# The mask of a block-causal attention moved from VectorE into the score matmuls, with a shifted schedule, in a float32 encoder block

## The reference

```
h = rms_norm(x); proj = h @ w_in
# A: 16 heads of 64, 2 kv heads, a window of two 64-token chunks, a sink per head, rotary
out_a = swa_sink_attention(rope(a_q), rope(a_k), a_v, sinks) * silu(a_g)
# B: 8 heads; q and kv from normed latents of 512 and 256; rotary part of 64 shared
s = (q_nope . k_nope + q_rope . k_rope) * scale
s = where(key_chunk <= query_chunk, s, -1e30)       # chunks of 64
out_b = softmax(s) @ v * silu(b_g)
y = rms_norm(x + concat(out_a, out_b) @ w_out) * final_norm_w
```

## Time and profile before

| | us |
|---|---|
| median of three runs | 681.09 (681.01 to 681.31) |
| the profiled execution | 681.09 |
| its span, first to last instruction | 679.3 |
| TensorE busy | 668.8 |
| VectorE, ScalarE, GpSimd busy | 336.6, 305.5, 307.2 |
| TensorE's granted clock, mean | 0.998 |

### The profile page before, as it was taken

One profiled execution on the slowest core, in us unless ns is written; L12 is line 12 of the kernel. 1 busy time (PEld: TensorE's weight loads), 2 busy tenths in 40 slices (PEclk: granted clock), 3 DMA queues, 4 the chain that ended last, 5 costly groups with the idle time before them and its releaser, 6 DMA issues.

```text
span 679.3 us, 8915 instructions
## 1 busy us (share of the span) xinstructions
PE 668.8 (98%) x3196; PEld 559.2 (82%) x3196; DVE 336.6 (50%) x596; ACT 305.5 (45%) x574; POOL 307.2 (45%) x149
## 2 busy tenths in 40 slices
PE   8999999999999999999999999999999999999995
PEld 7888888888888888888888888888888888888884
DVE  6857132988784635645554577778651100101013
ACT  7723231311343664565465466676753321313233
POOL 0044443354253532542443645556966584464720
PEclk9999999999999999999999999999999999999999
DMA  8632322223232212222321412102025732233225
GB/s 332 234 108 95 109 93 94 94 95 108 76 94 94 93 63 94 93 77 80 113 78 62 151 64 94 63 31 95 32 94 179 285 124 93 93 99 107 73 77 203
DMA packets 21878, 73.54 MB, mean 108 GB/s; under 512 B 2385, under 2 KB 2641, under 8 KB 21713
## 3 DMA queue, kind: packets, MB, share of 16 engines
q1 hardware_dynamic: 18144, 65.61, 28.4%
q10 hardware_dynamic: 3696, 7.43, 3.0%
HBM read 68.83 MB, written 4.19 MB: 108 GB/s over the span
## 4 chain that ended last, share of the span: by engine, by line
PE 91%; DVE 4%; ACT 2%; issue 1%; DMA 1%; SPq 0%; ACTq 0%; DVEq 0%
PE bank L1084 28%; PE bank L1080 28%; PE bank L1083 28%; PE bank L1212 1%; PE bank L1222 1%; PE bank L1331 1%; DVE bank L944 1%; DVE pb L953 1%; DVE t L909 1%; DMA xs<-x_t 1%; DVE ptb_lo L958 1%; PE bank L1234 1%; PE bank L1235 1%; PE bank L1100 1%; PE bank L1103 1%
## 5 line engine op out<-in xcount | busy, mean ns | idle before, releaser
L283 POOL TENSOR_TENSOR w_lo<-w_raw,w_hi 128x1024 fp32r<-128x1024 f32 x100 | 242.3, 2428 | 312.9 <-ACT w_hi L369 312.9
L369 ACT ACTIVATE w_hi<-w_raw 128x1024 fp32r<-128x1024 f32 x110 | 116.2, 1056 | 208.3 <-PE bank L1080 173.4
L1080 PE MATMUL bank<-x_hi,w_hi 128*128 128x512 f32 x504 | 196.9, 391 | 0.0
L1084 PE MATMUL bank<-x_lo,w_hi 128*128 128x512 f32 x504 | 196.7, 390 | 0.0
L1083 PE MATMUL bank<-x_hi,w_lo 128*128 128x512 f32 x504 | 196.2, 389 | 0.0
L1084 PEld LDWEIGHTS bank<-x_lo,w_hi 128*128 128x128 f32 x504 | 94.6, 188 | 20.2
L1080 PEld LDWEIGHTS bank<-x_hi,w_hi 128*128 128x128 f32 x504 | 94.7, 188 | 18.9 <-DVE mixed L894 0.5
L1083 PEld LDWEIGHTS bank<-x_hi,w_lo 128*128 128x128 f32 x504 | 94.7, 188 | 18.5
L1080 PE MATMUL bank<-w_hi,mx_hi 128*128 128x512 f32 x256 | 100.5, 393 | 0.0
L1083 PE MATMUL bank<-w_hi,mx_lo 128*128 128x512 f32 x256 | 100.0, 391 | 0.0
L1084 PE MATMUL bank<-w_lo,mx_hi 128*128 128x512 f32 x256 | 99.8, 390 | 0.0
(11 more groups left out here) (209 smaller groups left out, 923.3 us busy)
## 6 DMA issues: line engine op xcount, KB each, us to landing
w_raw<-w_stream SPq DMA_DIRECT2D x110, 512.0 KB, 3.3
y<-x_nat ACTq DMA_DIRECT2D x4, 1024.0 KB, 9.8
out<-y SPq DMA_DIRECT2D x6, 512.0 KB, 3.1
xs<-x_t SPq DMA_DIRECT2D x4, 512.0 KB, 5.3
mixed<-x_t SPq DMA_DIRECT2D x4, 512.0 KB, 5.1
fw<-final_w ACTq DMA_DIRECT2D x1, 1024.0 KB, 18.0
cos_b<-tables ACTq DMA_DIRECT2D x2, 256.0 KB, 2.9
sin_b<-tables ACTq DMA_DIRECT2D x2, 256.0 KB, 3.2
```

Source lines behind the costliest of these rows:

```text
L283: pool.tensor_tensor(w_lo[:, s % HL, :], w_raw[:, s % RAW, :], w_hi[:, s % HL, :].bitcast(F32), ALU.subtract)\
L369: act.activation(w_hi[:, s % HL, :], w_raw[:, s % RAW, :], ACT.Copy).then_inc(w_hi_ready, 1)
L1080: ins = pe.matmul(dst, ah, bh, start=start, stop=False)
L1084: return pe.matmul(dst, ah, bl, start=False, stop=stop)
```

## The change

The mask moves to TensorE: a sixth matmul adds to the last 64 columns of a score the product of a bf16 identity and a bf16 tile of 128x64 that holds -1e30 in its first 64 rows. VectorE then only reduces to the negated maximum. The two constants are made in the start stage, and the older mask tile with its two memsets ahead of B's first rotation is gone. Beside that the tables shift: A's group 0 has its scores at half steps 4, 7, 9, 12; B's chunks, rotations and mixed halves move by a fill or two; the rotary table load moves from fill 2 to fill 1; and the low halves of the query latent go from GpSimd to VectorE.

```diff
-AT_SCORES = [{2: 0, 5: 1, 8: 2, 11: 3}] * 4
-AT_TRANSPOSE = [{5: 0, 8: 1, 11: 2, 14: 3}] * 4
-AT_PV = [{7: 0, 10: 1, 13: 2, 16: 3}] * 4
+AT_SCORES = [{4: 0, 7: 1, 9: 2, 12: 3}] + [{2: 0, 5: 1, 8: 2, 11: 3}] * 3
+AT_TRANSPOSE = [{7: 0, 9: 1, 12: 2, 14: 3}] + [{5: 0, 8: 1, 11: 2, 14: 3}] * 3
+AT_PV = [{9: 0, 11: 1, 14: 2, 16: 3}] + [{7: 0, 10: 1, 13: 2, 16: 3}] * 3
-LATENT_AT = {9: 0, 10: 1, 12: 2, 13: 3}
+LATENT_AT, LATENT_LOW_AT = {9: 0, 10: 1, 12: 2, 13: 3}, {9: (0,), 10: (1,), 13: (2, 3)}
-B_CHUNKS = [{2: (5,), 4: (6,), 10: (7,)}, {1: (8,), 3: (9,), 10: (10,)}, {1: (11,), 3: (12,), 10: (13,)},
-            {1: (14,), 4: (15,), 6: (16,), 8: (17,), 10: (18,)}]
+B_CHUNKS = [{1: (5,), 3: (6,), 10: (7,)}, {1: (8,), 3: (9,), 10: (10,)}, {1: (11,), 3: (12,), 10: (13,)},
+            {1: (14,), 2: (15,), 4: (16,), 7: (17,), 9: (18,)}]
-B_ROTARY = [{3: (0,), 4: (1, 2), 5: (3,), 6: (4,), 7: (5,)}] + [{2: (0,), 3: (1,), 4: (2, 3), 5: (4,), 6: (5,)}] * 3
+B_ROTARY = [{3: (0, 1), 4: (2,), 5: (3,), 6: (4,), 7: (5,)}] + [{2: (0, 1), 3: (2,), 4: (3,), 5: (4,), 6: (5,)}] * 3
-M_AT = {3: 2, 5: 3, 7: 4, 9: 5, 10: 6}
+M_AT = {2: 2, 4: 3, 5: 4, 7: 5, 9: 6}
@@ gpsimd: the low halves of the latent leave its loop of chunks
-                for k in {PB0 + AHEAD - 4: (0,), PB0 + AHEAD - 3: (1,), PB0 + AHEAD - 2: (2, 3)}.get(c, ()):
-                    pool.wait_ge(cqs_split, k + 1)
-                    pool.wait_ge(lat_lo, 2 + k)
-                    pool.tensor_tensor(cqs_lo[:, k, :], cq[:, k, :], cqs_hi[:, k, :].bitcast(F32), ALU.subtract).then_inc(lat_lo, 1)
@@ scalar
-                act.activation(B[4 + u % 2][:, 0:n], B[4 + u % 2][:, 0:n], ACT.Exp, bias=st_b[:, u % 4, 0:1], scale=-1.0,
+                act.activation(B[4 + u % 2][:, 0:n], B[4 + u % 2][:, 0:n], ACT.Exp, bias=st_b[:, u % 4, 0:1],
-                        if p == 0 and f == 2:
+                        if p == 0 and f == 1:
                             act.wait_ge(gated, 8)
@@ vector
+            dve.memset(mask_bf[:, :], 0.0).then_inc(consts_set, 1)
+            dve.wait_ge(consts_set, 3)
             dve.memset(v_t[:, 0:CHUNK], 0.0)
+            dve.memset(mask_bf[0:64, :], MASK_VALUE).then_inc(consts_set, 1)
             dve.wait_ge(tables_landed, 48)
+            dve.tensor_copy(ident_bf[:, :], ident[:, :]).then_inc(consts_set, 1)
+                    for k in LATENT_LOW_AT.get(hf, ()) if t == 3 else ():
+                        dve.wait_ge(cqs_split, k + 1)
+                        dve.tensor_tensor(cqs_lo[:, k, :], cq[:, k, :], cqs_hi[:, k, :].bitcast(F32), ALU.subtract).then_inc(lat_lo, 1)
-                sc = B[4 + u % 2][:, 0:n]
-                dve.tensor_tensor_reduce(sc, sc, mask_b[:, SEQ - n:], -1.0, 3e38, ALU.add, ALU.min, st_b[:, u % 4, 0:1]).then_inc(b_max, 1)
+                dve.reduce_max(st_b[:, u % 4, 0:1], B[4 + u % 2][:, 0:n], AX.X, negate=True).then_inc(b_max, 1)
-            dve.memset(mask_b[:, :], 0.0).then_inc(b_mask, 1)
-            dve.wait_ge(b_mask, 1)
-            dve.memset(mask_b[0:CHUNK, SEQ - CHUNK:], MASK_VALUE).then_inc(b_mask, 1)
@@ tensor
+            pe.wait_ge(consts_set, 6)
-                three(dst, qn_hi[par][:, h, q], qn_lo[par][:, h, q], kn_hi[par][:, h, 0:n], kn_lo[par][:, h, 0:n], False, True).then_inc(b_scores, 1)
+                three(dst, qn_hi[par][:, h, q], qn_lo[par][:, h, q], kn_hi[par][:, h, 0:n], kn_lo[par][:, h, 0:n], False, False)
+                pe.matmul(B[4 + w % 2][:, n - CHUNK:n], ident_bf[:, :], mask_bf[:, :], start=False, stop=True).then_inc(b_scores, 1)
```

More of the change, by code:

```diff
@@ L143, in build @@
         ident = at("ident", [P, P], F32, region(512))
[L144 to L147, removed]
+        ones = at("ones", [P, P], F32, region(512))
+        fold = at("fold", [P, P], F32, region(512))
         r_sums = region(512)
@@ L150, in build @@
         fold_r = at("fold_r", [P, P], F32R, r_sums)
+        ident_bf = at("ident_bf", [P, P], BF16, region(256))
+        mask_bf = at("mask_bf", [P, CHUNK], BF16, region(128))
         st_a = at("st_a", [P, 2, 6, 4], F32, region(192))
@@ L242, in build @@
         b_rot_evac, b_rot, b_rot_hi, b_rot_lo = sem("b_rot_evac"), sem("b_rot"), sem("b_rot_hi"), sem("b_rot_lo")
-        b_mask, b_scores, b_max, b_exp, b_recip, b_probs = sem("b_mask"), sem("b_scores"), sem("b_max"), sem("b_exp"), sem("b_recip"), sem("b_probs")
+        b_scores, b_max, b_exp, b_recip, b_probs = sem("b_scores"), sem("b_max"), sem("b_exp"), sem("b_recip"), sem("b_probs")
         b_turned, b_pt_hi, b_pt_lo, b_pv, b_out = sem("b_turned"), sem("b_pt_hi"), sem("b_pt_lo"), sem("b_pv"), sem("b_out")
@@ L319, in _ @@
             assert (KR0 + 2) % HL == 0
-            with pool.Fori((KR0 + 2) // HL, b_head // HL - 1) as i:
+            with pool.Fori((KR0 + 2) // HL, b_head // HL) as i:
                 for s in range(HL):
                     low_part(HL * i + s, s)
-            for c in range(b_head // HL * HL - HL, b_head):
+            for c in range(b_head // HL * HL, b_head):
                 low_part(c, c)
-                for k in {PB0 + AHEAD - 4: (0,), PB0 + AHEAD - 3: (1,), PB0 + AHEAD - 2: (2, 3)}.get(c, ()):
-                    pool.wait_ge(cqs_split, k + 1)
-                    pool.wait_ge(lat_lo, 2 + k)
-                    pool.tensor_tensor(cqs_lo[:, k, :], cq[:, k, :], cqs_hi[:, k, :].bitcast(F32), ALU.subtract).then_inc(lat_lo, 1)
             for ct in range(2):
@@ L706, in _ @@
             dve.tensor_tensor(sin_r[:, :], sin_r[:, :], rstd[:, :], ALU.mult).then_inc(consts_set, 1)
-            dve.wait_ge(consts_set, 4)
+            dve.wait_ge(consts_set, 7)
             def rotate_terms(src, cos, sin, count, evac=proj_evac):
@@ L964, in b_take @@
                 dve.tensor_tensor(m, B[7][:, :], m, ALU.mult).then_inc(b_out, 1)
-            dve.memset(mask_b[:, :], 0.0).then_inc(b_mask, 1)
-            dve.wait_ge(b_mask, 1)
-            dve.memset(mask_b[0:CHUNK, SEQ - CHUNK:], MASK_VALUE).then_inc(b_mask, 1)
             for part in range(6):
                 b_rotary(0, part)
-            dve.wait_ge(b_mask, 2)
             b_tile_low(5)
```

## The result

The changed kernel takes 688.62 us (median of four runs, 687.51 to 689.06) against 681.09 (681.01 to 681.31): ratio 1.0107, 95% interval 1.0090 to 1.0126. Slower was right, the size was not: +3.0 us forecast, +7.5 measured, outside the range of 682.0 to 685.8.

The account below looks back on a forecast made before the run. TensorE's queue was taken as the bound. Masks 3.3, less 1.7 of old waits, plus 0.6 (A group 0), 0.5 (fill 1) and 0.3 (last pair) made +3.0: 684.1 us, range 682.0 to 685.8.

Parts of the forecast that it names:

- Latent low halves: Four subtractions moved to VectorE in A, at most 0.69 us each: done 0.3 before TensorE asks, so no cost.
- Masks, 3.3: 32 extra mask matmuls on TensorE in B's scores, about 0.11 us each on the longer ones: 3.1 to 3.5 in all.
- rival 2: Next weight load does not wait for the mask, which steps only 0.037 us: +0.9, 682.0 us; chance 0.13.
- the prediction's own sign of being wrong: A step of 0.04 us behind the masks in TensorE's queue, or waits of B as large as before.
- Old waits, 1.7 back: Seven TensorE waits in B, 1.78 us in all: shorter VectorE chains, moved rotation parts and later TensorE recover 1.7.
- My 0.7 against 0.50: Score 6 of pair 2: chain gains 0.3 from the moved rotation part, four masks give 0.4, against a 0.50 wait.
- A group 0, 0.6: First A group's new schedule: two new TensorE waits of 0.3 us at transpositions 1 and 3; bounds 0 and 1.4.
- Fill 1 of pair 0, 0.5, and the last pair, 0.3: Work moved on ScalarE in B makes TensorE wait at transposition 1 of pair 0 and transposition 3 of the last pair.
- Output stage unchanged: After B, the output stage was expected to stay the same whether the forecast was right or wrong.
- Constants, nothing: Memsets and one 128x128 VectorE copy in the start stage: no cost; bounds 0 and 0.7.
- Rival 1: B is held by the VectorE and ScalarE chain, masks fall into its waits: -1.2, 679.9 us; chance 0.07.
- Rival 3: Work moved on ScalarE costs more than the moved rotation gives, waits at upper bounds: +4.7, 685.8 us; chance 0.17.

Follow-up runs that it names:

- e1: Changed kernel with the four latent low halves back on GpSimd: 683.50 us, against 681.36 for the kernel before beside it.
- e2: Changed kernel with the latent low halves still on VectorE but at later half steps (11 and 14): 683.60 us, against 681.36 for the kernel before.
- e4: Changed kernel with GpSimd subtracting only 64 of 1024 columns in two weight chunks beside VectorE's two slow operations: 683.37 us, before 681.36.
- e3: Kernel before with only the latent low halves moved to VectorE, as in the change: 686.21 us, against 681.36 beside it.
- f1: Kernel before with only the mask moved to TensorE (all 32 scores, constants, reduction, sign), all tables as before: 681.06 us, against 681.11.
- g2: Kernel before with only the mask on TensorE and VectorE's table of rotation parts changed: 681.11 us, against 681.37 beside it.
- f3: Kernel before with only VectorE's table of rotation parts changed, no mask on TensorE: 682.25 us, against 681.11 beside it.
- f4: Kernel before with only B's fills changed (weight chunks, last pair's mixed halves, rotary table load in fill 1): 683.52 us, against 681.11.

## Why the prediction was wrong, step by step

- **Latent low halves, "Nothing, by 0.3; without that cover at most 0.7": the step that failed.** The arithmetic stood on 0.69 for the subtraction and 1.1 for the normalisation behind it. ScalarE was on time. The subtraction took 2.47 and the product of 128x4 2.29, 3.9 us more, less the cover of 0.3: 3.6, and 1.6 of lower clock behind it. 0.69 is VectorE's time with GpSimd out of the way. The step also says that GpSimd's earlier weight subtractions serve nobody who waits, and did not ask whom they hinder. GpSimd's timeline of before, which I had not laid beside it, has a subtraction at this very place, and the next one only the latent's low half away. Moved off GpSimd, that let the next one follow at once:

```profile
369.85 2.41 POOL L283 TENSOR_TENSOR w_lo<-w_raw,w_hi 128x1024 fp32r<-128x1024 f32 x1 [7.22 <-ACT w_hi L369]
372.22 1.29 POOL L329 TENSOR_TENSOR cqs_lo<-cq,cqs_hi 128x512 fp32r<-128x512 f32 x1
373.46 2.40 POOL L283 TENSOR_TENSOR w_lo<-w_raw,w_hi 128x1024 fp32r<-128x1024 f32 x1
```

  The trace of before even has a case of it. A 128x4 operation of VectorE that takes 0.16 at 366.69 takes 0.83 here, and it ends at 377.14 as GpSimd's ends at 377.12:

```profile
376.31 0.83 DVE L808 SCALAR_TENSOR_TENSOR st_a<-st_a,neg_sinks 128x4 f32<-128x4 f32 x1
375.82 1.30 POOL L329 TENSOR_TENSOR cqs_lo<-cq,cqs_hi 128x512 fp32r<-128x512 f32 x1
```

  e1, e2 and e4 show the cause, e3 that it needs nothing else of the change. The Trainium skill, "SBUF — State Buffer", Who interferes with whom, says that a VectorE instruction with two SBUF inputs contends with a GpSimd instruction that reads SBUF. The same section says that issue order decides who blocks. This case agrees: GpSimd started first both times, and VectorE's times went from 0.69 to 2.47 and from 0.16 to 2.29, while the low half at 239.38, which reads a bank, kept its 0.69 beside GpSimd.
- **Masks, 3.3:** 3.56, just over my 3.1 to 3.5. A mask steps 0.04, as rival 2 had it and as the prediction's own sign of being wrong, but the matmul behind it is 0.08 late. Rival 2 falls by that, and the step behind the mask alone was no good sign. The 24 longer scores cost 0.12 each and not 0.11, and the 8 short ones 0.6 together. That is near the 0.5 that the sum had by the rule of the Trainium skill, "TensorE: Matmul & The Clock Gate", Weight-path perf modes. The trace agrees with the rule: the bf16 load takes 0.10 and a 32-bit one 0.19.
- **Old waits, 1.7 back:** all came back, and 0.4 in the steps behind them that I had not counted, but it did not need the rotation parts to which I gave it. The masks alone do it (f1), and the table adds nothing beside them (g2). The table alone also empties scores 6, and makes as much and more elsewhere (f3). My 0.7 against 0.50 counted both; the two accumulator reads and TensorE's four masks were enough.
- **A group 0, 0.6:** the waits at transpositions 1 and 3 were 0.4 each, 0.8. What I left out is 0.5 where the group ends. The later group meets the query split, which GpSimd now holds up (3.8 us and not 2.8), and VectorE's take of the products and the gate's evacuation stand behind it. That this order makes the 0.5 is read from the trace and was not tested by itself. +1.3 to +1.4, at the upper bound.
- **Fill 1 of pair 0, 0.5, and the last pair, 0.3:** 0.6 and 0.3. Right, and by the order of work that was forecast; without the masks 1.3 and 0.8 (f4).
- **Output stage unchanged:** on TensorE yes; behind it -0.8, in no term of the sum.
- **Constants, nothing:** f1's first stretch shows none. What no term has is the 0.2 to 0.4 us that A and the 0.1 us that the output stage get shorter in each kernel with them; its cause stays open.

Without the failed step the sum 3.0 stood against 3.1 at e4's last matmul (its start is within 0.04 of before's), and e1, e2 and e4 came out 2.0 to 2.2 slower because of those 0.8. The sum of the rest was right partly by chance: masks and group 0 were 0.9 too low together, and what came back from the waits 0.6 too low. Rival 1 falls in f1, although the time stays: TensorE's B grew by 1.2, as the chain held only seven places, and the 1.2 came back outside B. Rival 3 had the size of part of the miss and the wrong cause.

## What to carry to other kernels

Before an operation moves to VectorE, look at what GpSimd runs at its new place, and take its worst time as its own plus that of the GpSimd operation under way; the next small operation with two inputs in SBUF can be caught by the following one. What stands ahead of a wait matters more than how busy the engine is: VectorE was at 50%. And a device worth having in a few places may be worth nothing everywhere: in B, 9 masks where a wait follows gave back 0.7 us and all 32 cost 1.2.

## What the runs showed of the hardware that was not expected

- An operation of 128x4 took 2.29 us instead of 0.16 beside a GpSimd subtraction, while reductions (0.68 each at 374.27 in the trace of before) and operations that read a bank (0.69 at 239.38) kept their time beside one.
- With the same wait of 3.6 us TensorE had a granted clock of 0.5, that is 1.2 GHz, for 3.4 us (changed kernel, from 1.1 us after the wait) or for 6.8 us (e3, from 0.8 us before its end). It cost 1.6 and 2.8 us. The shortest runs of both, with mean clocks of 0.998 and 0.997, may have had none of it: kernels without such a stretch have 0.996 to 0.999. e3's runs spread over 4.4 us and those of the kernel before beside it over 1.0. That the clock makes the spread is likely, and no second execution was profiled.
- The length of VectorE's program decided whether a packet of its code lies beside the last stores, and the traces with one end 0.1 to 0.8 us later behind the last matmul. The Trainium skill, "Runtime: NRT & Kernel Launch", Instruction fetch mechanics, has each sequencer fetch its code over a DMA queue of its own while it runs and calls the cost mostly hidden. Here it was likely not hidden beside the last stores; the kernels differ in more than the packet.
- A wait of TensorE ahead of a score cost 0.1 more than its length, in the step behind it (0.27 and not 0.17 at 384 columns, at three scores of before against f1).
